# A two-layer transformer block on one core: norms over whole blocks, the gates' products spread over the first mixer slot, and the mixer's steps moved to later places

## The reference, cut to what matters

```
h = swiglu(rmsnorm(x)*g, w_ffn1_in, w_ffn1_out);  x += 0.5*rmsnorm(h)*g      # FFN 1, inner width 2816
h = mixer(rmsnorm(x)*g);                          x += rmsnorm(h)*g          # conv half and mLSTM half
h = swiglu(rmsnorm(x)*g, w_ffn2_in, w_ffn2_out);  x += 0.5*rmsnorm(h)*g      # FFN 2
mod = silu(c) @ w_ada + b_ada;  shift, scale, gate = split(mod, 3)
h = rms_norm(x)*g*(1+scale) + shift;  proj = h @ w_in                        # 16-head stick-breaking attention, pooling
out = rms_norm(x + gate * (merged @ w_out)) * final_gain

rmsnorm(x) = x * rsqrt(mean(x*x over the 1024 features) + 1e-6)
mixer(xn): bg, cg, hc, q, k, v, o, ig, fg = split(xn @ w_in)
  conv half  : bg * (conv3(cg*hc) + bias)
  mLSTM half : 4 heads, forward and backward in time; log-sigmoid gates fg are summed along time,
               combined with ig and a running maximum, and weigh the products q.k; then a norm per head
               and sigmoid(o)
```

## Time and profile before

| | us |
|---|---|
| median of 3 runs | 1606.37 |
| the profiled execution | 1609.75 |
| its span, first to last instruction | 1608.1 |
| PE busy | 1551.2 (96%) |
| DVE busy | 801.1 (50%) |
| ACT busy | 585.5 (36%) |
| POOL busy | 209.4 (13%) |

### The profile page before, as it was taken

How to read it: one execution, slowest core, us unless ns; L and a number is a source line. 1 busy time by engine, 2 the same in 40 slices (tenths; PEclk the granted TensorE clock), 3 DMA queues, 4 the chain that set the end, 5 groups by cost and what they waited for, 6 DMA issues and landing times.

```text
span 1608.1 us, 18797 instructions
## 1 busy us (share of the span) xinstructions
PE 1551.2 (96%) x7157; PEld 1280.5 (80%) x7157; DVE 801.1 (50%) x890; ACT 585.5 (36%) x783; POOL 209.4 (13%) x228
## 2 busy tenths in 40 slices
PE   7999999997999998999999999799999999999997
PEld 6888888885887886788888887688888877888876
DVE  3434434326366745543344233777888865433244
ACT  5222222223465413422222223466666633222222
POOL 4555455103110002000000000100000000000001
PEclk9999999998899998999999999799999999999999
DMA  5544444231142231322322322022122232332321
GB/s 173 157 143 150 137 151 149 94 101 53 53 115 73 79 105 53 105 87 95 104 92 92 105 104 78 27 79 77 54 78 64 67 105 82 102 105 79 103 79 53
DMA packets 136071, 152.91 MB, mean 95 GB/s; under 512 B 3248, under 2 KB 123180, under 8 KB 136028
## 3 DMA queue, kind: packets, MB, share of 16 engines
q1 hardware_dynamic: 131580, 137.40, 27.1%
q0 software_dynamic: 4304, 14.88, 3.3%
q10 hardware_dynamic: 144, 0.04, 0.0%
HBM read 150.08 MB, written 2.23 MB: 95 GB/s over the span
## 4 chain that ended last, share of the span: by engine, by line
PE 62%; DVE 2%; POOL 1%; ACT 1%; issue 1%; POOLq 0%; ACTq 0%; DVEq 0%
PE ps L1572 19%; PE ps L1574 19%; PE ps L1573 19%; PE ps L1849 1%; POOL xT L530 1%; PE ps L1859 1%; PE ps L1832 1%; PE ps L1858 1%; PE ps L1831 1%; DVE acc L1048 1%; PE ps L1636 0%; POOL xT L585 0%; PE ps L1768 0%; DVE tt L1067 0%; PE ps L1833 0%
## 5 line engine op out<-in xcount | busy, mean ns | idle before, releaser
L1572 PE MATMUL ps<-ah,wh 128*128 128x512 f32 x1504 | 601.3, 400 | 15.9 <-DVE al L1040 9.3
L1574 PE MATMUL ps<-ah,wl 128*128 128x512 f32 x1504 | 590.1, 392 | 0.0
L1573 PE MATMUL ps<-al,wh 128*128 128x512 f32 x1504 | 589.3, 392 | 0.0
L1007 DVE TENSOR_TENSOR wl<-raw,wh 128x2048 fp32r<-128x2048 f32 x94 | 215.3, 2290 | 402.6 <-ACT wh L602 402.3
L602 ACT ACTIVATE wh<-raw 128x2048 fp32r<-128x2048 f32 x94 | 179.9, 1914 | 482.2 <-PE ps L1574 482.2
L1572 PEld LDWEIGHTS ps<-ah,wh 128*128 128x128 f32 x1504 | 285.5, 190 | 73.3 <-issue 11.6
L1574 PEld LDWEIGHTS ps<-ah,wl 128*128 128x128 f32 x1504 | 284.4, 189 | 60.5
L1573 PEld LDWEIGHTS ps<-al,wh 128*128 128x128 f32 x1504 | 285.0, 190 | 55.5
L1572 PE MATMUL ps<-rh,wh 128*128 128x512 f32 x352 | 136.9, 389 | 0.0
L1573 PE MATMUL ps<-rl,wh 128*128 128x512 f32 x352 | 136.9, 389 | 0.0
L1574 PE MATMUL ps<-rh,wl 128*128 128x512 f32 x352 | 136.9, 389 | 0.0
(11 more groups left out here) (284 smaller groups left out, 1690.4 us busy)
## 6 DMA issues: line engine op xcount, KB each, us to landing
raw<-in_w_ffn_in SPq DMA_DIRECT2D x43, 1024.0 KB, 5.1
raw<-in_w_ffn_out SPq DMA_DIRECT2D x22, 1024.0 KB, 4.8
raw<-in_w_in SPq DMA_DIRECT2D x36, 512.0 KB, 4.8
raw<-in_w_in SPq DMA_DIRECT2D x14, 1024.0 KB, 5.9
ada_raw<-in_w_ada POOLq DMA_DIRECT2D x24, 512.0 KB, 4.6
raw<-in_w_mix_in SPq DMA_DIRECT2D x10, 1024.0 KB, 5.3
raw<-in_w_mix_out SPq DMA_DIRECT2D x4, 1024.0 KB, 4.9
raw<-in_w_branch_a SPq DMA_DIRECT2D x4, 1024.0 KB, 4.9
```

Source lines behind the costliest of these rows:

```text
L1007: nc.vector.tensor_tensor(wl[n % 2][:], raw[n % 2][:], wh[n % 2][:].bitcast(fp32), ALU.subtract).then_inc(lo_done, 1)
L1572: nc.tensor.matmul(bank, w[0], m[0], start=start, stop=False)
L1573: nc.tensor.matmul(bank, w[0], m[1], start=False, stop=False)
L1574: return nc.tensor.matmul(bank, w[1], m[0], start=False, stop=stop)
```

## The change

- **Norms.** The matrix `mean` (128x128, every element 1/1024) replaces the column of ones in stages 0 to 6, so one matmul of 128x512 gives the mean of the squares, already spread over all partitions. ACT takes the root of the whole bank with eps as bias, DVE takes the reciprocal of 128x512 (`inverse_root`). `spread`, the two small DVE operations and the copy to `rstd` go. The number of squares that are added before the matmul differs by stage (`ADDS`); the others go to PE one by one.
- **Stage 2.** ACT squares each block right after making its `ah`, into `sq2`; two DVE additions fold 8 blocks to 2; `sums` moves from place 4 of slot 0 to place 2 of slot 1.
- **Gates.** `gates` j runs at place j of slot 0. Slot 0 writes banks 4 and 5.
- **Modulation.** `ada` 0 to 5 run before slot 0, in the gap while the norm is finished; 6 and 7 run at places 2 and 4 of slot 0.
- **Later steps.** Nearly all other mixer steps move three to six places later.
- The copy `h7` of the first bank and the table load of the root come ahead of the last `hi` and `lo` of a stage. The block order is [7, 6, 5, 4, 0, 1, 2, 3].

```diff
-ORDER = [7, 6, 4, 0, 1, 2, 3, 5]
+ORDER = [7, 6, 5, 4, 0, 1, 2, 3]
-MIXER = [(0, "qk", {0: [("gates",), ("ada", 0)], 1: [("ada", 1)], 2: [("ada", 2)], 3: [("ada", 3)], 4: [("ada", 4), ("sums",)],
-                    5: [("ada", 5)], 6: [("ada", 6), ("spread",)], 7: [("ada", 7), ("rows", 0)]}),
-         (0, "v", {3: [("rows", 1)]}),
-         (0, "cg", {1: [("S", 0, 0, 0), ("S", 0, 0, 1)], 2: [("S", 0, 0, 2), ("S", 0, 0, 3), ("rows", 2)],
-                    5: [("cols",)], 6: [("prep", 0, 0, 0)],
-                    7: [("vt", 0, 0), ("vt", 0, 1), ("prep", 0, 0, 1), ("weigh", 0, 0, 0)]}),
-         (0, "o", {0: [("weigh", 0, 0, 1)], 2: [("mm", 0, 0, 0), ("div", 0, 0, 0)], 3: [("S", 0, 1, 0)],
-                   4: [("mm", 0, 0, 1), ("S", 0, 1, 1), ("div", 0, 0, 1)], 5: [("S", 0, 1, 2), ("prep", 0, 1, 0)], ...
+GAP = 6
+MIXER = [(0, "qk", {0: [("gates", 0)], 1: [("gates", 1)], 2: [("gates", 2), ("ada", 6)], 3: [("gates", 3)], 4: [("gates", 4), ("ada", 7)],
+                    5: [("gates", 5)], 6: [("gates", 6)], 7: [("gates", 7), ("norm",), ("rows", 0)]}),
+         (0, "v", {2: [("sums",)], 3: [("rows", 1)]}),
+         (0, "cg", {2: [("S", 0, 0, 0), ("S", 0, 0, 1)], 3: [("S", 0, 0, 2), ("S", 0, 0, 3)], 5: [("rows", 2)]}),
+         (0, "o", {0: [("cols",)], 1: [("prep", 0, 0, 0)], 2: [("vt", 0, 0), ("vt", 0, 1), ("prep", 0, 0, 1), ("weigh", 0, 0, 0)],
+                   3: [("weigh", 0, 0, 1)], 5: [("mm", 0, 0, 0), ("div", 0, 0, 0)], 6: [("S", 0, 1, 0)],
+                   7: [("mm", 0, 0, 1), ("S", 0, 1, 1), ("div", 0, 0, 1)]}),
...
+         (0, "hc", {0: [("S", 1, 0, 0), ("S", 1, 0, 1)], 1: [("S", 1, 0, 2), ("hy", 0, 0), ("prep", 1, 0, 0)],
+                    2: [("S", 1, 0, 3), ("hy", 0, 1), ("prep", 1, 0, 1)], 3: [("weigh", 1, 0, 0), ("weigh", 1, 0, 1)],
+                    4: [("hz", 0, 0), ("hz", 0, 1)], 5: [("vt", 1, 0), ("vt", 1, 1)], 7: [("mm", 1, 0, 0), ("S", 1, 1, 0), ("div", 1, 0, 0)]}),
...
+ADDS = (6, 5, 1, 5, 6, 5, 0, 6)
...
+            def root(stage, bank):
+                act.wait_ge(sum_done, stage + 1)
+                nc.scalar.activation(rstd[:], ps[:, bank, :], ACT.Sqrt, bias=eps1[:]).then_inc(rstd_done, 1)
...
+            def inverse_root(stage):
+                dve.wait_ge(rstd_done, stage + 1)
+                chain.link(nc.vector.reciprocal(rstd[:], rstd[:]))
...
+            lo(S_MIX + 1)
+            dve.wait_ge(sq_done, 8 * 2 + 8)
+            chain.link(nc.vector.tensor_tensor(sq2[:, 0:4, :], sq2[:, 0:4, :], sq2[:, 4:8, :], ALU.add))
+            nc.vector.tensor_tensor(sq2[:, 0:2, :], sq2[:, 0:2, :], sq2[:, 2:4, :], ALU.add).then_inc(acc_step, 1)
...
+                elif kind == "norm":
+                    lo(S_MIX + 2)
+                    inverse_root(2)
...
+            def sums(stage, bank, parts=None):
+                adds = ADDS[stage]
...
+                if adds:
+                    pe.wait_ge(acc_step, ACC[stage] + adds)
+                    nc.tensor.matmul(ps[:, bank, :], mean[:], acc[:], start=True, stop=False)
+                for j in range(adds + 1 if adds else 0, KD):
+                    pe.wait_ge(sq_done, 8 * stage + j + 1)
+                    source = sq[:, j % 2, :] if adds else sq6(j)
+                    last = nc.tensor.matmul(ps[:, bank, :], mean[:], source, start=j == 0, stop=j == KD - 1)
...
+            pe.wait_ge(rstd_done, 2)
+            for j in range(GAP):
+                mixer_step("ada", j)
```

More of the change, by code:

```diff
@@ L709, in _, with gates_hi @@
             load_root(3)
[L710 to L716, removed]
+            def gates_hi():
+                load_root(0)
+                act.wait_ge(gpad, 1)
+                act.wait_ge(gates_in, 16 * 5)
+                for q in range(4):
+                    last = nc.scalar.activation(gh[:, :, 32 * q:32 * q + HEADS], gw[:, :, HEADS * q:HEADS * q + HEADS], ACT.Copy)
+                last.then_inc(gw_hi, 1)
+            ffn(0, 0, S_F1I, S_F1O, gates_hi)
             post_norm(1, 0, S_MIX - 1)
-            scaled_hi(1, 1, "norm_mix_pre")
-            squares(2, lambda j, k: None)
+            scaled_hi(1, 1, "norm_mix_pre", square=sq2)
             hi(S_MIX + 1)
@@ L730, in mixer_step @@
             def mixer_step(kind, *step):
-                if kind == "spread":
-                    root(2)
+                if kind == "norm":
+                    hi(S_MIX + 2)
+                    root(2, 7)
                 elif kind == "rows" and step[0] == 0:
@@ L1043, in add_squares @@
             def add_squares(stage):
[L1045 removed]
+                for j in range(1, ADDS[stage] + 1):
                     dve.wait_ge(sq_done, 8 * stage + j + 1)
@@ L1088, in post_norm, with ffn @@
                     after(KD - 1)
[L1089 to L1096, removed]
+            def ffn(f, stage, base_in, base_out, first):
                 r2 = rstd[:].unsqueeze(1).to_broadcast([P, 2, T])
@@ L1559, in _ @@
             gained(KD - 1)
-            variance(7, 7, spread=False)
+            dve.wait_ge(sum_done, 8)
+            chain.link(nc.vector.tensor_scalar(r4[:], ps[:, 7, 0:TB], 1.0 / D, EPS, ALU.mult, ALU.add))
+            nc.vector.reciprocal(r4[:], r4[:]).then_inc(var_done, 1)
+            dve.wait_ge(rstd_done, 8)
             for n in OUT_DVE:
@@ L1621, in last_slot, with token_sums @@
                 before()
-                sums(stage, 7)
-                for j in (6, 7):
-                    if whole_bank:
-                        whole_bank(j)
-            def sums(stage, bank):
+                if whole_bank:
+                    token_sums()
+                    whole_bank(6)
+                    whole_bank(7)
+                else:
+                    sums(stage, 7)
+            def sums(stage, bank, parts=None):
+                adds = ADDS[stage]
+                if parts:
+                    pe.wait_ge(acc_step, ACC[stage] + adds)
+                    for part in parts:
+                        last = nc.tensor.matmul(ps[:, bank, :], mean[:], part, start=part is parts[0], stop=part is parts[-1])
+                    last.then_inc(sum_done, 1)
+                    return
+                if adds:
+                    pe.wait_ge(acc_step, ACC[stage] + adds)
+                    nc.tensor.matmul(ps[:, bank, :], mean[:], acc[:], start=True, stop=False)
[3 more added lines that the diff above has]
+                    last = nc.tensor.matmul(ps[:, bank, :], mean[:], source, start=j == 0, stop=j == KD - 1)
+                last.then_inc(sum_done, 1)
+            def token_sums():
+                stage, bank = 7, 7
                 for step in range(2):
@@ L1638, in sums @@
                 last.then_inc(sum_done, 1)
-            def spread(stage, bank):
-                pe.wait_ge(rstd_done, stage + 1)
-                for b in range(TB):
-                    last = nc.tensor.transpose(ps[:, bank, b * P:(b + 1) * P], r4[:, b:b + 1].to_broadcast([P, P]), ident[:])
-                last.then_inc(rb_done, 1)
             def ffn(f, pre, stage, base_in, base_out, o):
@@ L1800, in _ @@
             last_slot(S_F2I - 1, (ah[:, 2:4, :], al[:, 2:4, :]), R_MO + 4, 1, 3, lambda: pe.wait_ge(h7_done, 2))
-            spread(3, 7)
             ffn(1, 2, 4, S_F2I, S_F2O, 2)
             pe.wait_ge(t_done, 8 * T_OF[5] + 3)
-            for j in range(5):
-                if j < 4:
-                    pe.wait_ge(sq_done, 8 * 6 + j + 1)
-                else:
-                    pe.wait_ge(acc_step, ACC[6] + 3)
-                source = sq6(j) if j < 4 else acc[:]
-                for b in range(TB):
-                    last = nc.tensor.matmul(ps[:, 4, b:b + 1], source[:, b * P:(b + 1) * P], ones[:, 0:1],
-                                            start=j == 0 and b == 0, stop=j == 4 and b == TB - 1)
-            last.then_inc(sum_done, 1)
-            spread(6, 4)
+            sums(6, 6)
             def att_step(step, r):
```

129 lines of the change are left out of this document (68 added, 61 removed), and 13 rows, old and new, of the table MIXER.

## The result

The kernel after takes 1637.45 us, the median of 4 runs (1636.5 to 1639.02), the kernel before beside it 1607.16: a ratio of 1.0187, 95% interval 1.0169 to 1.0205. The change makes the kernel 30 us slower; 1600 was forecast. The profiled execution took 1636.5 us, its span is 1634.8.

A forecast was written before the change was run, and what follows sets the result against it. PE, busy 96% of the span, was taken as the bound, so only its waits, low clock or removable work could give time. From the median 1606.37, -1.5 - 1.0 - 3.2 - 0.9 + 0.1 = -6.5 gave 1599.9; range 1589 to 1616.

The forecast's parts named there:

- Float32 product: Norm's matmul of 128x512 in full float32: two records of 0.44 to 0.45 us, taken as 0.9 us.
- Rival 4: Cheap float32 products of 0.45 us: 5.8 us gained in all, 1594; chance 0.41 together with the forecast.
- Reciprocal of 128x512: DVE's inversion in each whole-block norm: 0.69 us at a plain rate, 1.7 if 2 ns per element; 0.7 taken.
- rival 1: Slow reciprocal: gain gone at 2.0 us; at 4.4 us each, 1621. Chance 0.24 for 2 us or more.
- multiplier, 5: Reciprocal on the path five times, stages 1, 2, 3, 5, 6: each extra us costs 5.
- two more memsets: At the start, on POOL: 0.2 us each, hidden under the load of x, at most +0.2 us.
- Seam after FFN 1, slot 0: Norm 0.25 us earlier, `ada` hidden in 3.9 us, gates inside slot 0, which ends at 408.7 instead of 425.25.
- The mixer's chain: `zrow` at 415.5, 9.0 us earlier; steps then make PE wait 19.4 us in all, giving back most of the lead.
- slot 10 starts at 558.0: End of the mixer walk: slot 9's work ended at 559.45 before, so 1.5 us won of 14.7.
- rival 3: Clock falls in the mixer's new holes: three falls cost 6 us, 1606; chance 0.17 shared with a reciprocal near 1.7.
- Rival 2: Mixer keeps PE's lead, waits as short as before: -14.7 us replaces -1.5, 1587; chance 0.18.
- Seams after the mixer and before attention, stages 0 and 4: Shorter norms: -1.0 us after the mixer, -3.2 before attention, -0.45 in each of stages 0 and 4.

The follow-up runs named there:

- a_place_cheap: Kernel after with unused `room` cut from 32 to 24 columns and each 128x512 reciprocal replaced by a minimum with ones: 1611.93 us, 1.0019 of the kernel before.
- m_later: a_place_cheap with mixer steps from S on 3 places later, 16 at the end, slots bg 0 and o 1 exchanged: 1594.23 us, 0.9907 of the kernel before.
- a_cheap: Kernel after with each norm's 128x512 reciprocal replaced by an element-wise minimum with ones: 1621.63 us, 1.0079 of the kernel before.

## Why the prediction was wrong, by its own steps

- **Float32 product, 0.9 us.** Right: two records, and products in a row come 0.86 us apart. Rival 4 (0.45) falls. The root took 0.69, not 0.60.
- **Reciprocal of 128x512, "I take 0.7".** This is the term that failed first: 3.35 us, outside both of its bounds (0.69 and 1.7) and short of the 4.4 of rival 1's dear end. Between 4 and 512 columns that is (3351 - 178) / 508 = 6.2 ns per column, while a plain operation needs 1.03. At that rate the four columns alone would have given about 21 ns of excess; the row has 8, so its fixed part must be shorter than that of a plain operation, which a single size cannot show. The Trainium skill (VectorE: DVE Perf Modes, the walkthrough of the 8-slice pipeline) calls it an iterative divide with a repeat count of 8; the run gives about 6 times a plain column's time, not 8, and does not show whether the turns are the reason. The claim that "the trace speaks against it" was the error of reading: a difference of two fixed costs was taken for a rate.
- **Its multiplier, 5.** Measured 5.9 to 6.4 with the places of the kernel after, 5.4 with the later ones. Stages 0 and 4 count too: PE waited 1.73 and 0.78 us for the gate's bank. The text had seen this wait but not its size: "above 3 us would use it up" leaves next to nothing at 3.35, and in a_place_cheap PE waits 1.02 us in stage 0 with the stand-in at 2.38. The part of the reciprocal in the 37.5 us between forecast and result is 16 to 18: the 15.8 to 17.0 of the two pairs, and up to 1.0 for the wait that the stand-in left in stage 0.
- **Start, "two more memsets".** Here a cost was missed altogether: the constants' bytes. By moving the operands behind them they cost 8.5 us in one pair of runs, 11.3 in the other. No rival had it.
- **Seam after FFN 1, slot 0.** The order of events is right. In the kernel after slot 0 lasts about as long as forecast (19.6 us), and starts late by the reciprocal and what came before. It ended at 415.05 against 408.7; 425.25 before. "Hidden in PE's wait" holds for `ada` there only because the reciprocal makes the wait long: they take 4.18 us and PE is idle 3.39 behind them. With the cheap norm they fall into the low clock, take 6.27 instead of 3.9 and become what the gates wait for, 0.8 us late.
- **The mixer's chain.** With a cheap norm the waits were 18.3 us against 19.4, at the steps named; `zrow` came at 417.25 against 415.5, late by what slot 0 was late. The step that failed is the next one, "slot 10 starts at 558.0": the holes bring the low clock back. That was rival 3, priced 6 us, and 6 us is what the clock's mean shows. In the forecast they excluded each other, in the run both happened. Of the 8.8 us in a_place_cheap 1.7 lie ahead of slot 1 (`ada` and slot 0, above), 6.7 in slots 1 to 9, where PE is busy 6.6 us longer, and 0.4 behind them.
- **Rival 2, the lead kept (1587).** False as a forecast for this list of places, right as to what is possible: with later places PE idled little, and m_later, without the inversion, came to 1594.
- **Seams after the mixer and before attention, stages 0 and 4.** a_place_cheap: -1.1, -3.2 and -0.5, forecast -1.0, -3.2 and -0.45. Right. With the real reciprocal they become +1.5, +2.1 and, with the spacing, +4.1.

In sum, from 1600 to 1637.5: reciprocal 16 to 18, placement 8.5 to 11.3, the gap and the mixer 8.8. That is 33 to 38 for 37.5; kernels of different sets are compared in it, and the kernel before alone moved by 2 us between them.

## What to carry to other kernels

- The price of an iterative operation is not to be read from a tile where the fixed cost hides the rate: two sizes are needed, and with one size the range is wide.
- A new small constant moves every buffer allocated behind it. Put it last, or, as far as these four placements show, keep the operands that TensorE streams at a multiple of 128 bytes.
- Where a chain starts later against its slots, the places of its steps must follow by what PE gains and not by where they are free; a hole of 2.8 to 4.0 us on PE cost some 1.5 to 2.3 us more by the clock behind it.
- A mean over a group can hide one odd case: look at the single executions (here 0.69 six times and 2.38 once, with a mean of 0.94).
- Work that is to fill a gap is priced at the clock that it will have there. Six `ada` hid behind a slow norm and were the bound behind a fast one.

## What the runs showed of the hardware

- The start address of the moving operand (or its distance to the weights' address, which stayed at a multiple of 128) sets the rate of a 128x512 product at full clock: 0.2267 us at a multiple of 128 bytes, 0.2289 at 64 past it, 0.2333 at 32 or 96 past it. Busy share and granted clock show nothing of it; only the count of records in a window does (354, 351, 345 in 80 us).
- Reciprocal on DVE: 3351 ns for 128x512 (3346 to 3354 in the seven norms), 178 ns for 128x4.
- An element-wise minimum of two 128x512 operands on DVE: 0.69 us in six norms, 2.38 to 2.41 in the one where POOL worked on another tensor at the same time (a_cheap, a_place_cheap, m_later). The reciprocal of one operand kept its 3.35 us beside the same work of POOL. That POOL is the reason was not tested by itself.
- A one-column float32 product, two records: 4.18 us for 36 records at the full clock, 6.27 where the clock fell to 0.50 among them.
